# A hybrid decoder step on one core: keys and values of a cache page fetched in one transfer, with the pages and the second half's caches placed anew

## The reference, cut to what matters

```python
raw_k, raw_v = gather_pages(...)          # (request, 1024, C_KV, HEAD_DIM)
def phi(rows, pe, w1, w2):                # windows of 32 rows, every 16 rows
    blk = rows[:, idx] + pe[None, None, :, None, :]
    flat = jnp.moveaxis(blk, 3, 2).reshape(b, n_cmp, g, CMP_LEN * hd)
    return jax.nn.silu(flat @ w1) @ w2
kc, vc = rope(phi(raw_k, pe_k, wk1, wk2), end), phi(raw_v, pe_v, wv1, wv2)
o_cmp = softmax(q @ kc.T) @ vc            # compressed branch
o_slc = softmax(q @ k_slc[sel].T) @ v_slc[sel]   # selected blocks, from the same pages
```

## Time and profile before

| what | value |
|---|---|
| time, median of 3 runs | 919.99 us (919.67 to 920.89) |
| time of the profiled execution | 919.65 us |
| its span, first to last instruction | 918.0 us |
| TensorE busy | 898.1 us, 98% of the span |
| VectorE busy | 648.2 us, 71% |
| ScalarE busy | 453.9 us, 49% |
| GpSimd busy | 193.8 us, 21% |
| mean granted TensorE clock | 0.998 of full speed |

### The profile page before, as it was taken

The page is one execution under the profiler, slowest core; times in us unless marked ns, Lnnn a source line. Parts: engine busy times, 40 slices in busy tenths (PEclk is TensorE's granted clock), DMA queues, the critical chain, the costliest instruction groups (busy, mean ns, idle before and its releaser), DMA issues.

```text
span 918.0 us, 21372 instructions
## 1 busy us (share of the span) xinstructions
PE 898.1 (98%) x7904; PEld 836.8 (91%) x7904; DVE 648.2 (71%) x1449; ACT 453.9 (49%) x900; POOL 193.8 (21%) x321
## 2 busy tenths in 40 slices
PE   6999999999999999999999999999999999999997
PEld 6999998888888799999999998898888978999996
DVE  6999766677666467656769996676866565765664
ACT  6444665465443444334543447664654444443352
POOL 1200000347658300000000000013575771000000
PEclk9999999999999999999999999999999999999999
DMA  9762995735979873333675577765569799335321
GB/s 330 296 221 101 404 373 207 295 149 181 315 225 291 267 329 141 138 139 124 255 255 201 201 310 268 307 269 232 201 181 298 241 272 357 127 147 202 157 93 51
DMA packets 66359, 209.96 MB, mean 229 GB/s; under 512 B 12192, under 2 KB 49776, under 8 KB 56272
## 3 DMA queue, kind: packets, MB, share of 16 engines
q1 hardware_dynamic: 57200, 187.67, 55.9%
q0 software_dynamic: 8912, 20.92, 7.1%
q10 hardware_dynamic: 144, 0.01, 0.0%
HBM read 202.58 MB, written 41.36 MB: 266 GB/s over the span
## 4 chain that ended last, share of the span: by engine, by line
PE 89%; DVE 3%; ACT 2%; issue 2%; SPq 2%; DMA 1%; DVEq 0%; ACTq 0%
PE bank L1050 65%; PE bank L1310 8%; PE bank L1063 4%; SPq L874 2%; PE bank L1188 1%; PE bank L1180 1%; PE bank L1344 1%; PE bank L1217 1%; PE bank L1230 1%; PE bank L1441 1%; PE bank L1243 1%; ACT paged_r L1576 1%; DMA big<-in_w_tok 1%; PE bank L1412 1%; ACT kvp L1544 0%
## 5 line engine op out<-in xcount | busy, mean ns | idle before, releaser
L1822 DVE TENSOR_TENSOR big_r<-big,paged_r 128x1024 fp32r<-128x1024 f32 (+1 forms) x160 | 194.7, 1221 | 72.9 <-ACT paged_r L1576 72.0
L1050 PE MATMUL bank<-xnT_high_r,paged_r 128*128 128x288 f32 x768 | 231.7, 302 | 0.0
L1050 PE MATMUL bank<-xnT_r,paged_r 128*128 128x288 f32 x704 | 207.7, 295 | 0.0
L1050 PE MATMUL bank<-xnT_high_r,big_r 128*128 128x288 f32 x704 | 207.1, 294 | 0.0
L1576 ACT ACTIVATE paged_r<-big 128x1024 fp32r<-128x1024 f32 (+1 forms) x160 | 166.8, 1049 | 5.4 <-DMA big<-in_w_feat 2.7
L1050 PE MATMUL bank<-short_r,big_r 128*128 128x288 f32 x568 | 167.5, 295 | 0.0
L1050 PEld LDWEIGHTS bank<-xnT_high_r,paged_r 128*128 128x128 f32 x768 | 144.0, 187 | 4.4 <-issue 2.0
L1050 PEld LDWEIGHTS bank<-xnT_high_r,big_r 128*128 128x128 f32 x704 | 132.5, 188 | 0.0
L1050 PE MATMUL bank<-short_r,paged_r 128*128 128x288 f32 x440 | 131.2, 298 | 1.2 <-DVE big_r L1822 1.0
L1050 PEld LDWEIGHTS bank<-xnT_r,paged_r 128*128 128x128 f32 x704 | 132.3, 188 | 0.0
L1050 PE MATMUL bank<-kvp_r,paged_r 128*128 128x288 f32 x440 | 130.4, 296 | 0.0
(11 more groups left out here) (352 smaller groups left out, 1804.6 us busy)
## 6 DMA issues: line engine op xcount, KB each, us to landing
big<-in_w_tok SPq DMA_DIRECT2D x13, 2048.0 KB, 9.7
big<-in_w_feat SPq DMA_DIRECT2D x12, 2048.0 KB, 8.5
big<-in_w_gate SPq DMA_DIRECT2D x10, 2048.0 KB, 8.6
out_kept_dil<-in_cache_dil SPq DMA_DIRECT2D x16, 1020.0 KB, 13.0
paged<-in_pool SPq DMA_DIRECT2D x218, 64.0 KB, 4.3
big<-in_w_up SPq DMA_DIRECT2D x12, 1024.0 KB, 8.7
paged<-in_pool POOLq DMA_DIRECT2D x166, 64.0 KB, 4.6
big<-in_kv_win SPq DMA_DIRECT2D x4, 2048.0 KB, 9.0
```

The lines of the kernel that those rows point to most:

```text
L1050: last = mm(out, l, r, start=(c == 0 and i == 0), stop=(c == n - 1 and i == 2))
L1822: v.tensor_tensor(l_part[:, rest], full[:, rest], h_part[:, rest].bitcast(FP32), ALU.subtract)\
```

## The change

The selected kinds of a page come in pairs: keys and values side by side in one transfer of 128 KB, 1 KB per partition. There are thus 256 page transfers instead of 512. SP issues 136 of them (286 before), GpSimd 120 (226 before). Since keys and values of a request now arrive together, places go by pairs of requests and no more by kind: the first half's first pair goes to `paged1` after `feat 4`, its second pair to `paged0` after `feat 5`. The second half's caches move too: keys of mixer A (`kA 1`) from `big0` to `big2`, its values (`vA 1`) from `big2` to `paged1`. The first gate weight moves from `paged1` to `paged0`, and the order of the last loads changes.

```diff
-POOL_PAGES = 15
-POOL_PAGES_FIRST = 8
+POOL_PAGES = 4
+POOL_PAGES_FIRST = 2
...
+    big_slot = {("kA", 1): 2, ("vA", 1): 3}
...
-    loads = big_keys[0:-3] + [("kA", 1), ("vA", 1), ("win", 1), gate_keys[0]] + up_keys[0:2] + gate_keys[1:2]
+    loads = big_keys[0:-3] + [("kA", 1), ("vA", 1), ("win", 1)] + gate_keys[0:2] + up_keys[0:2]
...
+    PAGE_HALVES = [(paged[1], 0), (paged[1], 1), (paged[0], 0), (paged[0], 1), (big[0], 0), (big[0], 1), (big[2], 0), (big[2], 1),
+                   (long, 0), (x[:, :, :].rearrange("p k n -> p (k n)"), 0)]
+    PAGE_SLOTS = {}
+    for page_pair, slot0 in ((("cmp", 0, 0), 0), (("cmp", 0, 1), 2), (("cmp", 1, 0), 4), (("cmp", 1, 1), 2), (("slc", 0, 0), 6),
+                         (("slc", 0, 1), 0), (("slc", 1, 0), 8), (("slc", 1, 1), 4)):
+        PAGE_SLOTS |= {key: slot0 + i for i, key in enumerate(pair_of(*page_pair))}
...
-        kind, which, hb, h = key
-        if kind == "cmp" and hb == 0:
-            queue.wait_ge(*big_used(Now.layer, split_keys[which - 2]))
...
+        queue.wait_ge(*{("cmp", 0, 0): big_used(layer, split_keys[-2]), ("cmp", 0, 1): big_used(layer, split_keys[-1]),
+                        ("cmp", 1, 0): big_used(layer, ("kA", 0)), ("cmp", 1, 1): pages_used(layer, ("cmp", 0, b)),
+                        ("slc", 0, 0): big_used(layer, ("kA", 1)), ("slc", 0, 1): big_used(layer, ("vA", 1)),
+                        ("slc", 1, 0): PJ.is_full(("hid", 1, 0, 1)), ("slc", 1, 1): pages_used(layer, ("cmp", 1, 0))}[kind, hb, bp])
...
+            k = 2 * (kind == "slc")
+            src = a["pool"][layer, bass.ds(numbers[hb][b, i], 1), :, k:k + 2, :]
...
-                    at_key = {("vA", 0): both("cmp", 0, 0), ("kA", 1): both("cmp", 1, 0), ("vA", 1): both("cmp", 0, 1),
...
+                    at_key = {("vA", 0): pair_of("cmp", 0, 0) + pair_of("cmp", 0, 1), ("kA", 1): pair_of("cmp", 1, 0),
+                              ("win", 1): pair_of("cmp", 1, 1) + pair_of("slc", 0, 0),
+                              FIRST: pair_of("slc", 0, 1) + pair_of("slc", 1, 0) + pair_of("slc", 1, 1)}
...
-                    if key == ("gate", 0, 0):
-                        sp.wait_ge(*pages_used(layer, ("slc", 0, 0, 1)))
+                    if key == ("vA", 1):
+                        sp.wait_ge(*pages_used(layer, ("cmp", 0, 0)))
+                    elif key == FIRST:
+                        sp.wait_ge(*pages_used(layer, ("cmp", 1, 2)))
+                    elif key in up_keys[0:2]:
+                        sp.wait_ge(*pages_used(layer, ("slc", 0, 0)))
...
                     for pg in PG:
-                        act.wait_ge(*pg.is_full(("cmp", kind, hb, bp)))
+                        for page_key in pair_of("cmp", hb, bp):
+                            act.wait_ge(*pg.is_full(page_key))
```

More of the change, by code:

```diff
@@ L671, in high_used_by @@
         return None
[L672 to L678, removed]
+    pair_of = lambda kind, hb, bp: [(kind, hb, RB // 2 * bp + i) for i in range(RB // 2)]
+    page_keys = sum([pair_of(kind, hb, bp) for kind in ("cmp", "slc") for hb in range(HB) for bp in range(2)], [])
+    PAGE_HALVES = [(paged[1], 0), (paged[1], 1), (paged[0], 0), (paged[0], 1), (big[0], 0), (big[0], 1), (big[2], 0), (big[2], 1),
[4 more added lines that the diff above has]
+        PAGE_SLOTS |= {key: slot0 + i for i, key in enumerate(pair_of(*page_pair))}
+    CMP_PLACE = {(0, 0): (paged[1], paged_r[1]), (0, 1): (paged[0], paged_r[0]), (1, 0): (big[0], big_r[0]),
+                 (1, 1): (paged[0], paged_r[0])}
     def page_share(key, z):
[L681 to L685, removed]
+        n = POOL_PAGES_FIRST if key in pair_of("cmp", 0, 0) else POOL_PAGES
+        return [i for i in range(PAGES) if (i % 2 == 0 and i < 2 * n) == (z == 0)]
+    PG = [Ring(nc, f"pages_{who}", layered(page_keys), 10, by=16, parts=lambda key, z=z: len(page_share(key, z)),
+               free=False, slots=lambda key: PAGE_SLOTS[key])
           for z, who in enumerate(("pool", "sp"))]
@@ L690, in page_parts @@
         hb, kind, bp, lh = piece
-        low = piece_rows(paged_r[PAGE_SLOTS[("cmp", kind, hb)]], piece)
+        low = piece_rows(CMP_PLACE[hb, bp][1], piece)
         high = page_high[PIECES.index(piece) % 2].rearrange("p (m n) -> p m n", m=16)
@@ L820, in pages_used @@
     def pages_used(layer, key):
-        kind, which, hb, h = key
+        kind, hb, b = key
         if kind == "cmp":
-            return PJ.is_full(("hid", hb, which, h), layer)
-        return O.is_full(("o", "s", hb), layer) if which else SC.is_full(("sscore", hb, "slc1"), layer)
+            return PJ.is_full(("hid", hb, 1, b // 2), layer)
+        return O.is_full(("o", "s", hb), layer)
     SROWS = {"d4": (("A",), [(P * c, P) for c in range(4)]),
@@ L964, in _ @@
                     if key == FIRST:
-                        sp.dma_start(dst[:, 0:2048], src[:, 0:2048]).then_inc(first_half_in[0], 16)
+                        for h in range(2):
+                            half = slice(2048 * h, 2048 * (h + 1))
+                            sp.dma_start(dst[:, half], src[:, half]).then_inc(first_half_in[h], 16)
                     else:
```

69 lines of the change are left out of this document (29 added, 40 removed).

## The result

The changed kernel takes 951.45 us (median of 6 runs, 947.57 to 955.51); the kernel before, run beside it, 920.18 us (919.55 to 921.33). The ratio is 1.033, 95% interval 1.0313 to 1.0347: slower, and 31.3 us more where 11.5 were forecast. The profiled execution took 953.08 us, 33.4 above the profiled one of before.

What follows compares the result with a forecast made beforehand. The prediction took TensorE, busy 98% of the span, as the bound, so only its idle time could move. 919.65 + 10.4 + 1.0 + 0.4 - 0.3 = 931.15 us, plus 0.34 for the median, gave 931.5 us; range 925.5 to 938.

Steps and rivals of the forecast that it cites:

- Term A: At piece 2, pages land late, ScalarE's rounding delays the copy to PT and TensorE stands: 2 x 5.2 = 10.4 us.
- Edits at nothing: Parts booked at no cost, among them the second half's second-pair burst (`cmp 1 1`), landing by 273.0 us, and the up weights.
- The rival with the fallen clock: TensorE's clock falls to half around the piece 2 stall, costing 1.8 us per layer, 935.1 us in all; chance 0.32.
- Term B: At the second half's first cache scores, `kA 1` lands late in `big2`: 0.5 us, twice, 1.0 us.
- Term C: The first gate weight waits for piece 15's end and its rounding may run late: 0.2 us, twice, 0.4 us.
- The -0.3 for the page wait: In layer 0's request stage, TensorE's one idle wait caused by a page goes away: -0.3 us.
- The issues saved: 256 of 512 page issues removed from SP's and GpSimd's queues, which TensorE doesn't wait for except for 0.3 us.
- The lower-bound case: Piece 2's burst is not held up by `vA 0`: 2 x 2.3 to 2 x 3.3 us, 925.7 to 927.7 us; chance 0.22.
- the hidden case: All 16 transfers land before piece 2's rounding at 232.10 us, no stall, at best 914.4 us; chance 0.03.
- the stall off the path: ScalarE is late at piece 2 but TensorE's bank is free otherwise, 921 us; chance 0.05.

Runs made afterwards that it cites:

- e1: The changed kernel with SP issuing `vA 0` only after GpSimd's pages of the first half's second pair have landed; 21.6 us above the kernel before.
- e4: The changed kernel with each queue's `slc(0,0)` pages held until the other queue's `cmp 1 1` pages have landed; 30.3 us above the kernel before.
- e5: As e1, with the first burst's 16 transfers bringing only keys, 64 KB instead of 128 KB; 17.6 us above the kernel before.
- e9: As e6, with the second burst's (`cmp 1 1`) keys and values in separate 64 KB transfers, keys first; 12.6 us above the kernel before.
- e8: The kernel before, without the change, with ScalarE's rounding of piece 2 also waiting for the load `kA 1`; 32.5 us above the kernel before.
- e3: The changed kernel with piece 2's rounding and splitting moved to just ahead of piece 1, behind the copy to PT; 17.0 us above the kernel before.
- e6: The changed kernel with the edits of e1 and e3 together; 9.1 us above the kernel before.

## Why the prediction was wrong

The direction, the place and the chain of cause (ScalarE waits, the copy behind it is late, TensorE stands at its transposes) were as written. The size was not, and the time lies 13 us above the range.

**Term A** was 2 x 5.2 us with an upper bound of 7.4 a layer; it measured 10.3 and 9.2. The step that failed is "I take the middle of 4.1 and 6.1, 5.1 us" for the landing of GpSimd's tail beside `vA 0`, and its upper bound, "if they got through only when `vA 0` is done, that is 231.6 + 7.9". That case is what happened, but `vA 0`, sharing the DMA engines with the pages, took 11.0 us. The 7.9 had been measured where it was issued ahead of the pages (226.88 us in the earlier trace rows), not behind them; a bound made from a transfer's duration at another place in the queues was none. e1 shows the part: without `vA 0` the waits are 5.9 and 4.9 us, 5.4 on average. That this is near the 5.2 booked is luck, since 1.0 of the 5.2 was meant for the load: by its own rows the prediction had 4.2 us for pages alone and 1.0 for `vA 0` beside them, and the runs show 5.4 and 4.4. The Trainium skill ("DMA: Bandwidth & Descriptors", "Queues, rings and completion order") has each DMA engine take turns between the queues that have work, a packet at a time. The trace agrees in kind: SP's load and GpSimd's pages move together and end together (243.8 and 244.0 us); how the turns divide the bytes, no run here shows.

**"Edits at nothing", `cmp 1 1`**, failed by the same kind of step: from the last issue at 268.9 on, "landing 2.3 to 4.1 us later, at most 273.0". That is 8.3 us after the release at 264.74. Measured, the second burst's last page comes 11.3 us after its release (piece 7's end at 279.11, ScalarE's start at 290.39), 10.4 with the selected pages held back (e4), and e1's first burst takes 11.0 (227.87 to 238.84), with half the bytes 8.6 (e5, 226.49 to 235.12). I added the latency of 64 KB pages to the last issue, and 128 KB pages in a burst took longer: 5.8 us for e1's last. The bytes over the rate alone, 7.8 us at 268 GB/s (e1), would not have warned me, being less than 8.3; as an estimate, 2.3 us until the first page lands and then 7.8 for the bytes give 10.1, nearer to what was measured. The text had the right condition, "Landing more than 1 us later, it would cost": it landed 3.0 later and cost 2.2. e9 confirms the bytes. The two waits cost 4.5 us and, with the clock, 7.7.

**The clock.** The rival with the fallen clock, at 0.32 and 1.8 us a layer, is what happened, in both layers: 1.6 and 2.9 us behind the first wait, 1.6 and 1.6 behind the second. Its price was right but for the 2.9. That it would also be paid behind a second wait was not foreseen. The reason against it, that dense work up to the gap would protect the clock, was wrong. e8 shows it without the change.

**Term B** was 0.5 in each layer; it was 1.0 in layer 0 and nothing in layer 1. **Term C**: TensorE waits 0.43 us for the first gate weight's part against 0.4 before, so its 0.4 were nothing. The -0.3 for the page wait was right. The issues saved gave nothing, as booked.

**The lower-bound case, the hidden case and the stall off the path** are excluded by the 10.3 us. The coupling that the last denies was the prediction's firmest point, and e3 shows it: with the rounding moved, 14.3 us are gone.

What stays open: why the second wait grows to 3.8 us in layer 1 of e6, how much of what e5 leaves of the first wait is release, issues or latency, and how much of the wait for selected pages in e9 is due to the load of `win 1` ahead of them and how much to the doubled issues. None of the versions reaches the kernel before; the nearest, e6, is 0.7 to 1.1% above it.

## What to carry to other kernels

When a change fuses transfers, look at what each consumer needs first: half of the bytes in front of piece 2 were for piece 6, and the places, now by pairs instead of by kinds, made 2.1 MB due in 5.3 us that had been spread out before. Check a burst twice, by last issue plus latency, and by the latency of its first transfer plus the bytes over the rate that the trace shows for such transfers, and take the later (here the second gives 10.1 us and 10.4 to 11.3 were measured, so leave a margin); then ask which load that nobody needs yet is queued beside it. And see what stands in order behind the instruction that will wait: moving the wait behind work that doesn't need the data was worth more than any edit of the transfers, as long as the data come before the next step that does.

## Unexpected about the hardware

A short wait can cost 1.7 times its length. In the changed kernel the wait of 2.2 us at L1421 was followed by 3.4 us at half clock, 1.2 GHz, which lost 1.6 us. But the wait of 2.82 us in e3 was followed by none (first row below, clock 1.00), and that of 3.6 us in its layer 1 was (second row): the length of the wait alone does not decide it. Shorter waits show both cases too: behind 1.9 and 1.8 us in e1 the clock stayed at 1.00, behind 1.9 us in e4's layer 1 it fell.

```profile
240.00:250.00 10.00, 7.18 (x61) 1.00 0.66 223
...
698.00:710.00 12.00, 8.95 (x52) 0.72 0.38 123
```

The Trainium skill ("TensorE: Matmul & The Clock Gate", "HAM oscillation") describes such falls behind waits for DMA. The waits of 15.0 and 14.4 us in e8 agree; behind waits of 2 to 3 us the runs show falls in some places and none in others.
